# Column blocks and row blocks of the merge and the feed-forwards taken in batches of four and two

## The chip, the cores and the metric

One core of one Trainium2 chip runs the whole program. The metric is the device time of one execution in microseconds, the median of three runs. Engines are named as the profile names them: PE (TensorE, matmuls), PEld (its weight loads), DVE (VectorE), ACT (ScalarE), POOL (GpSimd), SP (the queue that starts the weight DMAs).

## The reference, cut to what matters

A block of 256 tokens with 1024 channels goes through three layers. What the change touches is the end of the first layer and the two feed-forwards of the others:

```
merged = (sigmoid(g_conv) * (yc @ w_out_conv)) + (sigmoid(g_attn) * (ya @ w_out_attn))   # first layer
out    = merged @ w_o                                                                 # 8 blocks of 128 columns
...
a, b = split(x @ w_in); a = causal conv of width 3 over tokens (a) + conv_b            # feed-forward, twice
out  = (gelu(a) * b) @ w_out                                                          # 22 blocks of 128 columns
```

All of it is f32. Each operand is split in a high and a low part (fp32r), and a product is three matmuls: high times high, low times high, high times low.

## The kernel before, in words

All weights come as one stream of 300 blocks, 128 partitions by 8 tiles of 128 columns (512 KB each), through a ring of three slots (`RING = 3`). For a block, SP starts the DMA into `raw[slot]`; ACT copies it rounded into `wh[slot]` (L396, `make_high`, once PE has used the block three before); DVE makes `wl = raw - wh` (L790, `make_low`); PE waits for that with `ready(b)`. The semaphore `used` counts the blocks that PE has finished. Every engine runs its list in order, so the refills of the ring (`refill`) are written between the other work of ACT and DVE by hand, and a refill waits where the list waits.

Two kinds of block matter here.

- A **column block** (`stationary`, L1363 to L1365) makes 128 columns of a product for all 256 tokens: 8 times three matmuls, each with its own weight load of 128 columns and 256 moving columns, into `bank[n][:, 0:256]`. Between two column blocks PE issues nothing else.
- A **row block** (`row`, `row_tile`, L1434 to L1436) multiplies a finished, activated block of 128 channels (`mh`, `ml`) with 128 rows of the output matrix: 12 matmuls of 512 moving columns, which add to the four banks 4 to 7 (`ysum`) over the whole stage.

The stages, in order. The **pairs stage** (`first(i)`, eight turns of a loop) has nine column blocks for a pair of heads: q, k, xc, then the scores, cg, bg, zc, then transposes, za, gc, then the products with the values (`pv`), ga. They go round three banks. ga is the last of a turn, q the first of the next. The **merge** has 8 products i, each of two column blocks (`mix(0)` into bank 0, `mix(1)` into bank 1) and a row block. The first **feed-forward** (f0) and the second (f1) have 22 products each: column block a(i) into bank 0, b(i) into bank 1, and row(i).

The order of the blocks in these three stages is a0, b0, then in a loop a(i+1), row(i), b(i+1), and at the end a, b and the last two rows (`last_rows`), whose second row waits until the last product is activated. a(i+1) waits until DVE has read bank 0 (`free_a`), row(i) until `ml` is made. Before the first a of the loop, four matmuls of zeros (`open_banks`, L1555) open the banks 4 to 7, since the row blocks only add. In a feed-forward a0 and b0 are made together (`two_stationary`). What lies between b(i) and row(i) is a chain: ACT `base` (L688), DVE two taps (L1270, L1273), ACT gelu (L694), DVE product with bank 1 (L1281), ACT `mh` (L698), DVE `ml` (L800). The merge has a shorter one: DVE L1040, L1047, L1051, ACT L512, DVE L1055.

During the first turns of a feed-forward, DVE also finishes the residual input (`tail_step`, four steps of 128x1024), after which POOL loads the next gains.

Of the kernel before, what the change touches and what calls it, by code (L numbers as in the profile page):

```python
# [25 lines left out]
P = 128  # L26
# [50 lines left out]
WARM_SETUP = 12  # L77
WARM_PAIR = 6
# [12 lines left out]
def slot_of(b):  # L91
    return b % RING
# [20 lines left out]
def build_program(nc, a):  # L113
    ctx = ExitStack()
    with ctx:
# [274 lines left out]
        def _(act):  # L390
# [123 lines left out]
            refill(0, B_MIX)  # L514
            refill(0, B_MIX + 1)
            merge(0)

            def products(i):
                for n in range(3):
                    refill(i, B_MIX + 2 + n)  # L520
                merge(i + 1)

            for n in range(2):
                products(n)
                if n == 0:
                    act.wait_ge(mem_in, 16)
                part = slice(n * KT // 2, (n + 1) * KT // 2)
                act.activation(memh[:, part, :], memf[:, part, :], ACT.Copy).then_inc(mem_h, 1)
            with act.Fori(2, KT - 2) as i:
                products(i)  # L530
            refill(KT - 2, B_MIX + 2)
            merge(KT - 1, 1)
            refill(KT - 2, B_MIX + 3)
            refill(KT - 2, B_MIX + 4)
# [150 lines left out]
            def ffn(ph, layer, b0):  # L685
                def base(i):

                    act.activation(t_a[:, :], bank[0][:, 0:T], ACT.Identity,  # L688
                                   bias=convf[:, layer, bass.ds(i, 1), 3], scale=convf[:, layer, bass.ds(i, 1), 2]
                                   ).then_inc(S[ph, "base"], 1)  # L690
# [5 lines left out]
                def high(i, buf=0):  # L696
                    act.wait_ge(S[ph, "m"], i + 1)
                    act.activation(mh[:, buf, :], t_c[:, :], ACT.Copy).then_inc(S[ph, "mh"], 1)  # L698

                act.wait_ge(used, b0 + 1)  # L700
                base(0)
                refill(0, b0)
                gelu(0)
                refill(0, b0 + 1)
                high(0)

                def body(i):
                    bb = b0 + 2
                    act.wait_ge(used, i * RING + (bb + 1))
                    base(i + 1)  # L710
                    refill(i, bb)
                    gelu(i + 1)
                    if isinstance(i, int):
                        high(i + 1, 1)
                        refill(i, bb + 1)
                    else:
                        refill(i, bb + 1)
                        act.wait_ge(used, i * RING + (bb + 3))
                        high(i + 1)
                    refill(i, bb + 2)  # L720

                with act.Fori(0, FT - 2) as i:
                    body(i)
                body(FT - 2)
# [59 lines left out]
        def _(dve):  # L784
# [251 lines left out]
            def part_c(i, b):  # L1036
                dve.wait_ge(used, b)
                if isinstance(i, int):
                    dve.wait_ge(S["p1", "free_act"], 5 * PAIRS1 + 5)
                dve.scalar_tensor_tensor(out=t_a[:, :].unsqueeze(1), in0=gates[:, 0, bass.ds(i, 1), :], scalar=1.0,  # L1040
                                         in1=bank[0][:, 0:T].unsqueeze(1), op0=ALU.add, op1=ALU.mult
                                         ).then_inc(S["p2", "free_a"], 1)

            def part_a(i, b, buf=0):
# [3 lines left out]
                                                 scalar=1.0, in1=bank[1][:, 0:T].unsqueeze(1),  # L1048
# [4 lines left out]
                dve.sem_inc(S["p2", "m"], 1)  # L1053
                dve.wait_ge(S["p2", "mh"], i + 1)
                dve.scalar_tensor_tensor(out=ml[:, buf, :], in0=t_c[:, :], scalar=0.5, in1=mh[:, buf, :].bitcast(F32),  # L1055
                                         op0=ALU.mult, op1=ALU.subtract).then_inc(S["p2", "ml"], 1)

            part_c(0, B_MIX + 1)
            refill(0, B_MIX)
            part_a(0, B_MIX + 2)  # L1060
            refill(0, B_MIX + 1)
            def products(i):
                part_c(i + 1, i * RING + (B_MIX + 3))
                refill(i, B_MIX + 2)
                refill(i, B_MIX + 3)
                part_a(i + 1, i * RING + (B_MIX + 5))
                refill(i, B_MIX + 4)

            for n in range(3):
                products(n)  # L1070
                if n:
                    part = slice((n - 1) * KT // 2, n * KT // 2)
                    dve.wait_ge(mem_h, n)
                    low(meml[:, part, :], memf[:, part, :], memh[:, part, :].bitcast(F32), mem_l)
            with dve.Fori(3, KT - 2) as i:
                products(i)
            part_c(KT - 1, B_KM0 - 3)
            refill(KT - 2, B_MIX + 2)
            part_a(KT - 1, B_KM0 - 2, 1)
            refill(KT - 2, B_MIX + 3)  # L1080

# [182 lines left out]
            def ffn(ph, layer, b0, nm):  # L1264
                cf = Chain(dve, dchf[layer], 1)

                def taps(i):
                    cf.begin(i)
                    dve.wait_ge(S[ph, "base"], i + 1)
                    cf.link(dve.scalar_tensor_tensor(out=t_a[:, 1:T], in0=bank[0][:, 0:T - 1],  # L1270
                                                     scalar=convf[:, layer, bass.ds(i, 1), 1], in1=t_a[:, 1:T],
                                                     op0=ALU.mult, op1=ALU.add))
                    dve.scalar_tensor_tensor(out=t_a[:, 2:T], in0=bank[0][:, 0:T - 2],  # L1273
# [4 lines left out]
                def gated(i, b, buf=0):  # L1278
                    dve.wait_ge(used, b)
                    dve.wait_ge(S[ph, "g"], i + 1)  # L1280
                    dve.tensor_tensor(t_c[:, :], bank[1][:, 0:T], t_b[:, :], ALU.mult).then_inc(S[ph, "m"], 1)  # L1281
                    dve.wait_ge(S[ph, "mh"], i + 1)
                    low(ml[:, buf, :], t_c[:, :], mh[:, buf, :].bitcast(F32), S[ph, "ml"])

                taps(0)
                refill(0, b0)
                gated(0, b0 + 2)
                refill(0, b0 + 1)

                def body(i, last=False):  # L1290
                    taps(i + 1)
                    refill(i, b0 + 2)
                    if last:
                        gated(i + 1, i * RING + (b0 + 4), 1)
                        refill(i, b0 + 3)
                    else:
                        refill(i, b0 + 3)
                        gated(i + 1, i * RING + (b0 + 5))
                        refill(i, b0 + 4)

                for n in range(4):
                    body(n)
                    tail_step(nm, n)
                with dve.Fori(4, FT - 2) as i:
                    body(i)
                body(FT - 2, True)
# [52 lines left out]
        def _(pe):  # L1359
            def stationary(slot, out, mov_h, mov_l, k0=0, k1=KT):  # L1360

                for k in range(k0, k1):
                    pe.matmul(out, wh[slot][:, k, :], mov_h(k), start=k == 0, stop=False)  # L1363
# [81 lines left out]
            def last_rows(b, first, second, half, second_made=()):  # L1445

                ready(b + 1)
                row_tile(slot_of(b), *first, 0, False, False)
# [74 lines left out]
            def first(i):  # L1523
# [28 lines left out]
            def open_banks():  # L1552

                for n in range(4):
                    pe.matmul(bank[4 + n][:, :], zeros[:, 0:P], zeros[:, :], start=True, stop=False)  # L1555


            def mix(which, slot, bk):
                stationary(slot, bk[:, 0:T], lambda k: mixh[:, which, k, :], lambda k: mixl[:, which, k, :])

            pe.wait_ge(dch1, 6 * PAIRS1)
            pe.wait_ge(S["p1", "free_act"], 5 + 5 * PAIRS1)
            open_banks()
            ready(B_MIX + 1)
            mix(0, slot_of(B_MIX), bank[0])
            ready(B_MIX + 2)
            mix(1, slot_of(B_MIX + 1), bank[1])
            with pe.Fori(0, KT - 2) as i:
                ready(i * RING + (B_MIX + 3))
                pe.wait_ge(S["p2", "free_a"], i + 1)  # L1570
                mix(0, slot_of(B_MIX + 2), bank[0])
                ready(i * RING + (B_MIX + 4))
                pe.wait_ge(S["p2", "ml"], i + 1)
                row(slot_of(B_MIX + 3), mh[:, 0, :], ml[:, 0, :], False, False)
                ready(i * RING + (B_MIX + 5))
                mix(1, slot_of(B_MIX + 4), bank[1])
            ready(B_KM0 - 3)
            pe.wait_ge(S["p2", "free_a"], KT - 1)
            mix(0, slot_of(B_KM0 - 4), bank[0])
            ready(B_KM0 - 2)  # L1580
            pe.wait_ge(S["p2", "ml"], KT - 1)
            mix(1, slot_of(B_KM0 - 3), bank[1])
            last_rows(B_KM0 - 2, (mh[:, 0, :], ml[:, 0, :]), (mh[:, 1, :], ml[:, 1, :]), S["n1", "half"],
                      ((S["p2", "ml"], KT),))
# [175 lines left out]
            def finish(ph, main, r0, half):  # L1760
# [21 lines left out]
                last_rows(r0 + 6, (oh[:, 6, :], ol[:, 6, :]), (oh[:, 7, :], ol[:, 7, :]), half, ((S[ph, "ol"], 2),))  # L1782
# [5 lines left out]
            def ffn(ph, b0, nm):  # L1788
                two_stationary(b0, nm)
                open_banks()  # L1790

# [254 lines left out]
```

## Time and profile before

| | us |
|---|---|
| median of 3 runs | 978.41 (978.02 to 979.07) |
| the profiled execution, its own time | 979.72 |
| its span, first to last instruction | 978.1 |
| PE busy | 943.0 |
| DVE busy | 664.0 |
| ACT busy | 528.0 |
| pairs stage, start of q to end of ga | 38.5 to 259.5 |
| merge | 260.6 to 329.2 |
| f0, from its first row block on | 488.9 to 665.7 |
| f1, from its first row block on | 791.7 to 968.0 |

Matmuls are pipelined, so a matmul's own duration (0.28 us for 256 columns) is longer than its distance to the next one. In what follows the distance from start to start is what counts. The granted clock of TensorE is given as a share of full speed; in each of the four stages of the table it is 1.00.

### The profile page before, as it was taken

How to read it: one execution, taken by the hardware profiler on the slowest of the kernel's cores; microseconds unless marked ns; L12 is line 12 of the kernel's file. 1: busy time of each engine (PE TensorE's matmuls, PEld its weight loads, DVE VectorE, ACT ScalarE, POOL GpSimd, SP SyncE). 2: the span in 40 equal slices, each digit the busy share in tenths (PEclk: the TensorE clock that was granted, in tenths of full speed). 3: DMA queues.
4: the chain of work that ended last, by engine and by line, in shares of the span. 5: the costliest groups of instructions: out<-in, count | busy, mean ns of one | idle time of the engine just before them, and what ended most of it. 6: DMA issues, size and time to landing. Idle time of an engine off the chain costs nothing.

```text
span 978.1 us, 19996 instructions
## 1 busy us (share of the span) xinstructions
PE 943.0 (96%) x6998; PEld 855.9 (88%) x7006; DVE 664.0 (68%) x1258; ACT 528.0 (54%) x967; POOL 65.9 (7%) x119
## 2 busy tenths in 40 slices
PE   7999999999999989989999999999999999999995
PEld 4899999999999977667899999997998689999995
DVE  5566666566666866885877666667577777666665
ACT  5455555555444557774654555556566555555552
POOL 1000000000000001560100000001000100000001
PEclk9999999999999999999999999999999999999998
DMA  7555555556555466323456655555555445655552
GB/s 246 176 184 175 187 176 177 183 167 235 181 185 188 151 205 200 111 64 105 168 186 208 208 182 189 193 190 161 198 181 164 153 150 197 219 187 192 192 183 75
DMA packets 48227, 172.90 MB, mean 177 GB/s; under 512 B 6031, under 2 KB 6479, under 8 KB 48060
## 3 DMA queue, kind: packets, MB, share of 16 engines
q1 hardware_dynamic: 44732, 159.78, 49.3%
q0 software_dynamic: 3456, 12.61, 4.3%
q8 instruction: 24, 0.39, 0.2%
q14 instruction: 15, 0.12, 0.0%
HBM read 171.29 MB, written 1.07 MB: 176 GB/s over the span
## 4 chain that ended last, share of the span: by engine, by line
PE 84%; DVE 6%; DMA 4%; ACT 2%; issue 2%; POOL 0%; SPq 0%; POOLq 0%; ACTq 0%; DVEq 0%
PE bank L1363 18%; PE bank L1364 17%; PE bank L1365 17%; PE ysum L1434 6%; PE ysum L1436 6%; PE ysum L1435 6%; DMA sb_raw<-in_stream 4%; DVE sb_wl L790 2%; PE bank L1481 2%; PE ysum L1488 2%; ACT sb_wh L396 1%; PE ysum L1495 1%; PE ysum L1411 1%; PE ysum L1412 1%; PE ysum L1415 1%
## 5 line engine op out<-in xcount | busy, mean ns | idle before, releaser
L790 DVE TENSOR_TENSOR sb_wl<-sb_raw,sb_wh 128x1024 fp32r<-128x1024 f32 x300 | 365.6, 1223 | 152.7 <-ACT sb_wh L396 151.5
L1363 PE MATMUL bank<-sb_xh,sb_wh 128*128 128x256 f32 x1360 | 383.4, 282 | 1.8 <-DVE sb_t_a L1273 1.4
L396 ACT ACTIVATE sb_wh<-sb_raw 128x1024 fp32r<-128x1024 f32 x300 | 314.8, 1054 | 126.3 <-PE ysum L1436 51.4
L1364 PE MATMUL bank<-sb_xl,sb_wh 128*128 128x256 f32 x1360 | 380.0, 279 | 0.0
L1365 PE MATMUL bank<-sb_xh,sb_wl 128*128 128x256 f32 x1360 | 380.0, 279 | 0.0
L1363 PEld LDWEIGHTS bank<-sb_xh,sb_wh 128*128 128x128 f32 x1360 | 256.2, 188 | 10.6 <-issue 4.0
L1365 PEld LDWEIGHTS bank<-sb_xh,sb_wl 128*128 128x128 f32 x1360 | 258.1, 190 | 0.0
L1364 PEld LDWEIGHTS bank<-sb_xl,sb_wh 128*128 128x128 f32 x1360 | 255.3, 188 | 1.6
L1434 PE MATMUL ysum<-sb_wh,sb_mh 128*128 128x512 f32 x208 | 81.4, 391 | 1.9 <-DVE sb_ml L800 1.2
L1436 PE MATMUL ysum<-sb_wh,sb_ml 128*128 128x512 f32 x208 | 80.9, 389 | 0.0
L1435 PE MATMUL ysum<-sb_wl,sb_mh 128*128 128x512 f32 x208 | 80.9, 389 | 0.0
L698 ACT ACTIVATE sb_mh<-sb_t_c 128x256 fp32r<-128x256 f32 x44 | 18.3, 416 | 89.5 <-DVE sb_t_c L1281 89.5
L688 ACT ACTIVATE sb_t_a<-bank,sb_convf 128x256 f32<-128x256 f32 x44 | 24.9, 566 | 47.6 <-PE bank L1365 45.1
L433 ACT ACTIVATE sb_pr<-sb_sc,sb_mx 128x128 f32<-128x128 f32 x80 | 35.5, 445 | 22.7 <-DVE sb_mx L920 22.7
L1434 PEld LDWEIGHTS ysum<-sb_wh,sb_mh 128*128 128x128 f32 x208 | 39.0, 188 | 9.5 <-issue 3.4
L1436 PEld LDWEIGHTS ysum<-sb_wh,sb_ml 128*128 128x128 f32 x208 | 39.0, 188 | 8.2
L1435 PEld LDWEIGHTS ysum<-sb_wl,sb_mh 128*128 128x128 f32 x208 | 39.0, 188 | 6.1
L1363 PE MATMUL bank<-sb_mixh,sb_wh 128*128 128x256 f32 x128 | 36.2, 282 | 0.0
L1364 PE MATMUL bank<-sb_mixl,sb_wh 128*128 128x256 f32 x128 | 36.0, 281 | 0.0
L1365 PE MATMUL bank<-sb_mixh,sb_wl 128*128 128x256 f32 x128 | 36.0, 281 | 0.0
L800 DVE TENSOR_TENSOR sb_ml<-sb_t_c,sb_mh 128x256 fp32r<-128x256 f32 x44 | 18.7, 426 | 24.2 <-ACT sb_mh L698 24.2
L1270 DVE SCALAR_TENSOR_TENSOR sb_t_a<-bank,sb_convf,sb_t_a 128x255 f32<-128x255 f32 x44 | 21.2, 481 | 18.3 <-ACT sb_t_a L688 18.2
(265 smaller groups left out, 1343.9 us busy)
## 6 DMA issues: line engine op xcount, KB each, us to landing
sb_raw<-in_stream SPq DMA_DIRECT2D x300, 512.0 KB, 3.4
sb_bias<-rel_rows POOLq DMA_DIRECT2D x12, 384.0 KB, 3.8
sb_bias<-in_alibi POOLq DMA_DIRECT2D x8, 256.0 KB, 3.1
sb_gb<-in_ln_g POOLq DMA_DIRECT2D x4, 512.0 KB, 4.8
sb_gb<-in_ln_b POOLq DMA_DIRECT2D x4, 512.0 KB, 6.5
sb_x_tok<-in_x SPq DMA_DIRECT2D x2, 512.0 KB, 3.8
sb_memf<-in_mem_t POOLq DMA_DIRECT2D x1, 1024.0 KB, 8.4
out<-sb_x_tok SPq DMA_DIRECT2D x2, 512.0 KB, 2.6
```

What stands on the lines that cost most here:

```text
L396: act.activation(wh[slot][:, :, :], raw[slot][:, :, :], ACT.Copy).then_inc(split_h, 1)
L433: act.activation(to[:, branch, h, cols], src, ACT.Exp, bias=mx[:, c:c + 1], scale=-1.0, accum_out=den[:, c:c + 1]).then_inc(S[ph, "exp"], 1)
L688: act.activation(t_a[:, :], bank[0][:, 0:T], ACT.Identity, bias=convf[:, layer, bass.ds(i, 1), 3], scale=convf[:, layer, bass.ds(i, 1), 2] ...
L790: dve.tensor_tensor(wl[slot][:, :, :], raw[slot][:, :, :], wh[slot][:, :, :].bitcast(F32), ALU.subtract).then_inc(split_l, 1)
L1270: cf.link(dve.scalar_tensor_tensor(out=t_a[:, 1:T], in0=bank[0][:, 0:T - 1], scalar=convf[:, layer, bass.ds(i, 1), 1], in1=t_a[:, 1:T], op ...
L1363: pe.matmul(out, wh[slot][:, k, :], mov_h(k), start=k == 0, stop=False)
L1364: pe.matmul(out, wh[slot][:, k, :], mov_l(k), start=False, stop=False)
L1365: last = pe.matmul(out, wl[slot][:, k, :], mov_h(k), start=False, stop=k == KT - 1)
L1434: pe.matmul(out, th[:, t * P:(t + 1) * P], hw, start=start, stop=False)
L1435: pe.matmul(out, th[:, t * P:(t + 1) * P], lw, start=False, stop=False)
L1436: last = pe.matmul(out, tl[:, t * P:(t + 1) * P], hw, start=False, stop=stop)
L1481: last = pe.matmul(outs[h][:, cols], q[r, t * P:(t + 1) * P], k[r, 0:lead + (t + 1) * P], start=True, stop=True)
```

## The change

The order becomes: four column blocks a(2j), b(2j), a(2j+1), b(2j+1) into banks 0 to 3, then row(2j-1), then row(2j). The stream of weights is laid out in that order. `open_banks` goes; the first row block starts its banks itself (`start=True`). The first batch of the merge waits, bank by bank, only for what last read that bank, and no longer for all of the pairs stage. The first matmul of some column blocks is issued as two: in the first block of every later batch as 192 and 64 columns, and in every ga of the pairs stage as 128 and 128. On DVE the making of `ml` is a step of its own, after the refill that follows the product; on ACT the odd product's `mh` waits in every batch but the first for the row block of the last odd product. The first two batches of a feed-forward hold the four tail steps, one for each product.

```diff
+SPLIT = 192
...
-            def stationary(slot, out, mov_h, mov_l, k0=0, k1=KT):
+            def stationary(slot, out, mov_h, mov_l, k0=0, k1=KT, split=0):
                 for k in range(k0, k1):
-                    pe.matmul(out, wh[slot][:, k, :], mov_h(k), start=k == 0, stop=False)
+                    if split and k == 0:
+                        pe.matmul(out[:, 0:split], wh[slot][:, k, :], mov_h(k)[:, 0:split], start=True, stop=False)
+                        pe.matmul(out[:, split:T], wh[slot][:, k, :], mov_h(k)[:, split:T], start=False, stop=False)
+                    else:
+                        pe.matmul(out, wh[slot][:, k, :], mov_h(k), start=k == 0, stop=False)
...
-                    stationary(slot_of(B_FIRST + p), bank[p % 3][:, 0:T], xm, xml)
+                    stationary(slot_of(B_FIRST + p), bank[p % 3][:, 0:T], xm, xml, split=P if kind == "ga" else 0)
...
+            def batches(ph, b0, count, column, half):
+                def column_free(i, n):
+                    if n > 1:
+                        pe.wait_ge(S[ph, "free_a" if n == 2 else "m"], i)
+                def row_made(b, i, c, start=False):
+                    ready(b)
+                    pe.wait_ge(S[ph, "ml"], i + 1)
+                    row(slot_of(b0 + (4 if start else 4 - c)), mh[:, c, :], ml[:, c, :], start, False)
+                def four(j):
+                    for n in range(4):
+                        ready(j * 6 + (b0 + n))
+                        column_free(j * 2, n)
+                        column(n, slot_of(b0 - 1 + n), SPLIT if n == 0 else 0)
+                row_made(b0 + 5, 0, 0, True)
+                with pe.Fori(1, count // 2 - 1) as j:
+                    four(j)
+                    row_made(j * 6 + (b0 + 4), j * 2 - 1, 1)
+                    row_made(j * 6 + (b0 + 5), j * 2, 0)
+                four(count // 2 - 1)
+                row_made(b0 + 3 * count - 2, count - 3, 1)
+                last_rows(b0 + 3 * count - 2, (mh[:, 0, :], ml[:, 0, :]), (mh[:, 1, :], ml[:, 1, :]), half,
+                          ((S[ph, "ml"], count - 1),), ((S[ph, "ml"], count),))
+            p1a, p1d = S["p1", "free_act"], S["p1", "free_dve"]
+            for n, made in enumerate((((dch1, 6 * PAIRS1 - 1), (p1d, 4 * PAIRS1 + 5)),
+                                      ((dch1, 6 * PAIRS1), (p1a, 5 * PAIRS1 + 4)),
+                                      ((p1a, 5 * PAIRS1 + 5),), ())):
...
+                mix(n % 2, slot_of(B_MIX + n), bank[n])
+            batches("p2", B_MIX, KT, lambda n, slot, split: mix(n % 2, slot, bank[n], split), S["n1", "half"])
...
             def ffn(ph, b0, nm):
                 two_stationary(b0, nm)
-                open_banks()
...
+                pe.wait_ge(kv_free, 4)
+                for n in range(2, 4):
+                    ready(b0 + n + 1)
+                    stationary(slot_of(b0 + n), bank[n][:, 0:T], xm, xml)
+                batches(ph, b0, FT, lambda n, slot, split: stationary(slot, bank[n][:, 0:T], xm, xml, split=split),
+                        S["n3", "half"])
```

DVE's list in a feed-forward afterwards (ACT's is alike: `base`, refill, gelu, refill, `mh`, and after the odd product two more refills):

```diff
+                def products(j):
+                    fixed = isinstance(j, int)
+                    b = b0 if fixed and j == 0 else b0 - 1
+                    for c in range(2):
+                        i = j * 2 + c
+                        taps(i, c)
+                        refill(j, b + 2 * c, 6)
+                        gated(i, j * 6 + (b + 2 * c + 2), c)
+                        refill(j, b + 2 * c + 1, 6)
+                        gated_low(i, c)
+                        if c:
+                            refill(j, b + 4, 6)
+                            if not fixed or 0 < j < FT // 2 - 1:
+                                refill(j, b + 5, 6)
+                        if fixed and j < 2:
+                            tail_step(nm, 2 * j + c)
```

## Rows read from the trace of the kernel before

**Rows 1.** The page: busy time of the engines over the span, and instructions.
```profile
PE 943.0 (96%) x6998; PEld 855.9 (88%) x7006; DVE 664.0 (68%) x1258; ACT 528.0 (54%) x967; POOL 65.9 (7%) x119
```

**Rows 2.** Busy by stretch, f0: window, length, PE, PEld, DVE, ACT, POOL, PEclk, DMA, GB/s.
```profile
488.00:661.00 173.00, 172.17 (x1234) 162.25 (x1233) 116.15 (x151) 89.66 (x127) 1.13 (x2) 1.00 0.59 194
```

**Rows 3.** Timeline of PE, pairs stage: first matmuls of consecutive blocks (start, duration).
```profile
41.30 0.28 PE L1363 MATMUL bank<-sb_xh,sb_wh 128*128 128x256 f32 x1
44.02 0.28 PE L1363 MATMUL bank<-sb_xh,sb_wh 128*128 128x256 f32 x1
...
65.91 0.28 PE L1363 MATMUL bank<-sb_xh,sb_wh 128*128 128x256 f32 x1
68.74 0.28 PE L1363 MATMUL bank<-sb_xh,sb_wh 128*128 128x256 f32 x1
```

**Rows 4.** Timeline of PE, f0: a block, the next block, the row block.
```profile
567.66 0.28 PE L1363 MATMUL bank<-sb_xh,sb_wh 128*128 128x256 f32 x1
...
570.49 0.28 PE L1363 MATMUL bank<-sb_xh,sb_wh 128*128 128x256 f32 x1
...
573.32 0.39 PE L1434 MATMUL ysum<-sb_wh,sb_mh 128*128 128x512 f32 x1
```

**Rows 5.** Timeline of PE, f0: a block that starts after an idle stretch, its follower.
```profile
536.97 0.38 PE L1363 MATMUL bank<-sb_xh,sb_wh 128*128 128x256 f32 x1 [0.38 <-DVE sb_wl L790]
537.19 0.28 PE L1364 MATMUL bank<-sb_xl,sb_wh 128*128 128x256 f32 x1
...
539.81 0.39 PE L1434 MATMUL ysum<-sb_wh,sb_mh 128*128 128x512 f32 x1
```

**Rows 6.** The chain of waits, merge: start, duration; eight transposes of 128 columns.
```profile
334.73 0.87 PE ysum L1470 x8
```

**Rows 7.** Timeline of PE, scores: matmuls of 128 columns of unsplit f32.
```profile
46.83 0.37 PE L1481 MATMUL bank<-sb_k_s,sb_q_s 64*128 64x128 f32 x1
...
47.04 0.27 PE L1481 MATMUL bank<-sb_k_s,sb_q_s 64*128 64x128 f32 x1
```

**Rows 8.** Timeline of PE, from the last ga into the merge.
```profile
259.41 0.28 PE L1365 MATMUL bank<-sb_xh,sb_wl 128*128 128x256 f32 x1
260.56 0.81 PE L1555 MATMUL ysum<-sb_zeros 128*128 128x512 bf16 x3 [0.87 <-ACT sb_gates L501]
...
261.33 0.28 PE L1364 MATMUL bank<-sb_mixl,sb_wh 128*128 128x256 f32 x1
```

**Rows 9.** Timeline of PE, last two row blocks of the merge and of f0.
```profile
323.94 0.39 PE L1436 MATMUL ysum<-sb_wh,sb_ml 128*128 128x512 f32 x1
...
325.30 0.39 PE L1435 MATMUL ysum<-sb_wl,sb_mh 128*128 128x512 f32 x1
...
661.01 0.39 PE L1436 MATMUL ysum<-sb_wh,sb_ml 128*128 128x512 f32 x1
...
661.87 0.39 PE L1435 MATMUL ysum<-sb_wl,sb_mh 128*128 128x512 f32 x1
```

**Rows 10.** Timeline, start of f0: PE's zeros, DVE, first row block.
```profile
483.23 1.23 DVE L790 TENSOR_TENSOR sb_wl<-sb_raw,sb_wh 128x1024 fp32r<-128x1024 f32 x1
483.75 0.55 PEld L1555 LDWEIGHTS ysum<-sb_zeros 128*128 128x128 bf16 x4
...
489.24 0.39 PE L1435 MATMUL ysum<-sb_wl,sb_mh 128*128 128x512 f32 x1
```

**Rows 11.** Timeline, start of f1: DVE, PE's last matmuls of a0 and b0, first row block.
```profile
785.97 1.23 DVE L790 TENSOR_TENSOR sb_wl<-sb_raw,sb_wh 128x1024 fp32r<-128x1024 f32 x1
786.08 0.63 PE L1381 MATMUL bank<-sb_xl,sb_wh 128*128 128x256 f32 x4
...
792.04 0.39 PE L1435 MATMUL ysum<-sb_wl,sb_mh 128*128 128x512 f32 x1
```

**Rows 12.** The page's groups: ACT's part of a refill (count, busy us, mean ns).
```profile
L396 ACT ACTIVATE sb_wh<-sb_raw 128x1024 fp32r<-128x1024 f32 x300 | 314.8, 1054 | 126.3 <-PE ysum L1436 51.4 <-PE bank L1365 32.6 <-DMA sb_raw<-in_stream 25.1
```

**Rows 13.** Busy by stretch, early (columns as in rows 2), where the granted clock was low.
```profile
20.00:23.30 3.30, 3.30 (x9) 2.59 (x8) 1.42 (x2) 0.00 (x0) 0.00 (x0) 0.50 0.74 263
```

More of the change, by code:

```diff
@@ L512, in merge @@
                 act.activation(mh[:, buf, :], t_c[:, :], ACT.Copy, scale=0.5).then_inc(S["p2", "mh"], 1)
[L514 to L525, printed above, removed]
-                    act.wait_ge(mem_in, 16)
[L527 to L534, printed above, removed]
+            for j in range(KT // 2):
+                b = 6 * j + B_MIX - (j > 0)
+                refill(0, b)
+                refill(0, b + 1)
+                merge(2 * j, 0)
+                refill(0, b + 2)
+                refill(0, b + 3)
+                if j:
+                    act.wait_ge(used, b + 5)
+                merge(2 * j + 1, 1)
+                refill(0, b + 4)
+                if j:
+                    refill(0, b + 5)
+                if j == 0:
+                    act.wait_ge(mem_in, 16)
+                if j < 2:
+                    part = slice(j * KT // 2, (j + 1) * KT // 2)
+                    act.activation(memh[:, part, :], memf[:, part, :], ACT.Copy).then_inc(mem_h, 1)
             def refills(b0, n):
@@ L1282, in gated @@
                     dve.wait_ge(S[ph, "mh"], i + 1)
[L1283 to L1306, printed above, removed]
+                    low(ml[:, c, :], t_c[:, :], mh[:, c, :].bitcast(F32), S[ph, "ml"])
+                def products(j):
+                    fixed = isinstance(j, int)
[8 more added lines that the diff above has]
+                        if c:
+                            refill(j, b + 4, 6)
+                            if not fixed or 0 < j < FT // 2 - 1:
+                                refill(j, b + 5, 6)
+                        if fixed and j < 2:
+                            tail_step(nm, 2 * j + c)
@@ L1308, in _ @@
+                for j in range(2):
+                    products(j)
+                with dve.Fori(2, FT // 2 - 1) as j:
+                    products(j)
+                products(FT // 2 - 1)
             ffn("f0", 0, B_FFN0, "n2")
@@ L1443, in row, with last_rows @@
                 last.then_inc(used, 1)
-            def last_rows(b, first, second, half, second_made=()):
+            def last_rows(b, first, second, half, first_made=(), second_made=()):
                 ready(b + 1)
+                for made in first_made:
+                    pe.wait_ge(*made)
                 row_tile(slot_of(b), *first, 0, False, False)
@@ L1550, in _ @@
             first(PAIRS1 - 1)
[L1552 to L1562, printed above, removed]
-            open_banks()
-            ready(B_MIX + 1)
@@ L1565, in _ @@
[L1565 to L1584, printed above, removed]
+            def mix(which, slot, bk, split=0):
+                stationary(slot, bk[:, 0:T], lambda k: mixh[:, which, k, :], lambda k: mixl[:, which, k, :],
+                           split=split)
@@ L1905, in skewed @@
     def skewed(n, first, second, rows):
[L1906 to L1914 removed]
+        for j in range(0, n, 2):
+            for i in (j, j + 1):
+                add(_columns(first, i * P))
+                add(_columns(second, i * P))
+            for i in (j - 1, j):
+                if i >= 0:
+                    add(rows[i * P:(i + 1) * P])
         add(rows[(n - 1) * P:n * P])
```

149 lines of the change are left out of this document (61 added, 88 removed).

## The prediction

> **What bounds the kernel.** I read the busy times of the page first: PE is busy for 943.0 of 978.1 us, DVE for 664.0 and ACT for 528.0 [rows 1]. Only what shortens PE's list or fills its gaps can move the time. The busy times by stretch say the same of a feed-forward: PE 172.17 of 173.00 us, DVE 116.15, ACT 89.66, granted clock 1.00 [rows 2]. So inside the loops there is almost no wait to take away, and what the change can win lies (a) in how densely PE's matmuls follow each other, and (b) in the gaps at the seams of the stages. For (a) the view is the timeline of PE with its starts. A column block of 24 matmuls comes in two lengths: 44.02 - 41.30 = 2.72 us and 68.74 - 65.91 = 2.83 us, with the same instructions, tiles and clock [rows 3]. I call them fast (113 ns a matmul) and slow (118 ns). The reader is to see that nobody waits for another engine in either: it is a rhythm between weight loads and matmuls, and it stays as it is from block to block until something disturbs PE. In the feed-forward the block behind a row block is slow, and the one after it: 570.49 - 567.66 and 573.32 - 570.49, both 2.83 [rows 4]. That row stands for 46 such seams in merge, f0 and f1; none of them leads into a fast block. In the pairs stage ga, q, k, xc are slow (ga starts behind the value products) and cg to gc fast (behind the scores or the transposes).
>
> **The change part by part** (against the profiled execution, 979.72 us; it is 1.31 above the median of 978.41, which I take off at the end).
>
> *Seam into the merge.* Before, PE's last ga matmul starts at 259.41, the zeros wait 0.87 for ACT's gates, and the second mix matmul starts at 261.33 [rows 8]. Two steps of 0.12 would have brought it to 259.65. The new first mix block waits only for the last low part of the convolution and for bank 0, both long done. Gain 1.68. Next late: the weights of the third block, since ACT refills that slot only behind ga; its two copies take 1.05 [rows 12] and 1.23 us and end some 3 us behind ga, and two blocks of 2.72 cover them.
>
> *Start of f0 and f1.* Before, from the zeros' weight load at 483.75 to the second matmul of row(0) at 489.24 it takes 5.49 us [rows 10], for a column block (2.83) and one row matmul (0.23): 2.43 too long, by the zeros, the wait for DVE's taps and that for `ml`. Now a1 and b1 follow at once into free banks. What is late next is a1's weights: DVE makes them from 483.23 to 484.46 [rows 10]. That is 0.71 behind 483.75; with the hand-over of 0.08 and a restart, which costs 0.22 instead of 0.12 for the first step [rows 5], 0.89 stays lost. Gain 1.54. In f1 the last of four matmuls from 786.08 ends its slot at 786.55, row(0) is at 792.04, DVE ends at 787.20 [rows 11]: 2.43 before, 0.65 + 0.18 = 0.83 after, gain 1.60. DVE gets a tail step of 1.2 us between the first and second product; following its list by hand, the weights of a2 are then done within 0.3 us of the time at which PE wants them. I leave that at nothing, and keep 0 to 0.3 for each.
>
> *Ends.* The last row block waits for the chain of the last product: 325.30 - 323.94 = 1.36 where two row matmuls take 0.45, so 0.91 in the merge, and 0.86 - 0.45 = 0.41 in f0 [rows 9]; f1 repeats f0 (a gap of the same 0.41 at its end). Now a whole row block (2.72) lies between. The chain takes longer, since ACT's `mh` waits for that row block: about 3.8 us behind b, against 4.1 when PE wants it. Gain 0.91 + 0.82 = 1.73, between 1.4 and 1.73.
>
> The seams give 1.68 + 1.54 + 1.60 + 1.73 = 6.55 us.
>
> *In the loops* the same instructions are issued in another order. Cover for the refills: a slot has two blocks of PE (5.4 us) from its release; ACT's copy, DVE's subtraction and the elementwise work before them end some 3 us (column) to 3.3 us (row block, whose `mh` now stands ahead) after it. Nothing waits. The one wait for weights in f0's loop (0.38 named, [rows 5]) comes with a gains load; it may stay or go: 0, bounds -0.5 and +0.5. The moved `ml` feeds a row block at least two column blocks later.
>
> *The split matmuls.* There are 8 in the pairs, 3 in the merge, 10 in each feed-forward: 31. No row shows an fp32r matmul below 256 columns, so I bound it. From below: every matmul has its own weight load, and transposes of 128 columns, each with one, follow at 0.87 / 8 = 0.109 us [rows 6]; two pieces cost 0.22 instead of 0.12, +0.10. From above: a narrow unsplit f32 matmul at 0.21 (47.04 - 46.83, [rows 7]), two pieces 0.42, +0.30. I take 0.10, because the loads are the same as the transposes'. The other end: 31 x 0.20 = 6.2 us more.
>
> The Trainium skill, "TensorE: Matmul & The Clock Gate", section "Back-to-back issue gap", gives N / 2.4 + 2.5 ns for a matmul alone; by it the pieces of 192 and 64 columns would take 112 ns together and the splits would be free, some 3 us less than my sum. The same page's "LDWEIGHTS" gives 107 ns for 128 columns, and the 0.109 of the transposes agrees with that, not with the first formula.
>
> *What the split does to the rhythm* is the largest term. Behind a row block the first matmul finds its weights loaded long ago, and the run falls into the slow rhythm, 46 times of 46. A narrow first piece ends before the next load does, so PE starts the following matmul right behind a load, as after an idle stretch. Such restarts mostly lead to the fast rhythm: 539.81 - 537.19 = 2.62 us for 23 matmuls in f0, 114 ns each [rows 5]. In the pairs all 16 starts behind scores and transposes are fast and all 8 behind the value products slow; of 24 other restarts in the timeline 17 are fast. Two kinds of split, each with one place and one outcome: I take both as working. Then ga, q, k, xc become fast: 8 + 7 x 3 = 29 blocks. The merge has 16 (the first batch follows ga, without a row block between), f0 40 and f1 41 that are now slow. 126 x 0.11 = 13.9 us. Off go 31 x 0.10 for the pieces and 31 x 0.04 for settling and for the first row matmuls behind a fast block: 4.3. Net 9.6. Bounds: if no split works, the loss is 3.1. Batches of four matter here only since they need half as many splits.
>
> Sum: 6.5 + 9.6 = 16.1. 979.72 - 16.1 = 963.6; at the median 978.4 - 16.1 = 962.3.
>
> **Rivals.** *Only the 192/64 split works:* 93 x 0.11 - 23 x 0.14 - 8 x 0.10 = 6.2, with the seams 12.7: 965.7. *Only ga's works:* 33 x 0.11 - 8 x 0.14 - 23 x 0.10 = 0.2, with the seams 6.7: 971.7. Against both: neither has a precedent in the trace, and ga starts where 8 of 8 are slow. *No split works,* a change that doesn't do what its split says: 6.5 - 3.1 = 3.4: 975.0. For it: a third of the restarts are slow, and the steps that decide differ by a few ns. *Slower: narrow pieces are dear and don't change the rhythm.* Each costs 0.30 [rows 7], 31 of them 9.3 against 6.5: 981.2. It decides from 0.21 us a split on; for it speaks the only narrow matmul not a transpose, against it the loads, which set the pace of transposes of the same width.
>
> *The clock falls in the batches.* Four banks in turn instead of two, with a fresh group in each. The trace has the low level of 1.2 GHz at 20.0 to 23.3, behind a wait: 9 row-sized matmuls in 3.30 us [rows 13], 0.41 apart as I count it, against 0.23 at 2.4 GHz. One such stretch in each of 26 batches costs 26 x 3.3 x (1 - 0.23 / 0.41) = 38 us: about 1000. Against it: the pairs stage goes round three banks with the clock at 1.00, and in the new loops PE never waits. The Trainium skill names this mechanism in the same page's section "A second HAM failure mode: psum-queue depth-cycling"; this trace doesn't bear it out.
>
> **How the numbers follow.** Both splits work 0.52; only 192/64 0.12; only ga's 0.12; none 0.16; slower by dear pieces 0.06; clock 0.02. The forecast is 962.3, its own range 960 to 964.5. To hold 8 in 10 the range must reach over the partial cases to that without rhythm: 960 to 975.5. About 0.2% (2 us) is what a measurement here tells from no change. Faster by more than that: all of the first three and most of the fourth, 0.89; within 0.2%: 0.04; slower: 0.07.
>
> **What would show it.** Timeline of PE: column blocks 2.72 us apart in merge and feed-forwards, a batch of six blocks 16.5 instead of 16.75; the two pieces 0.11 apart each; a turn of the pairs stage 27.4 instead of 27.66. No zeros; the first mix matmul 0.12 behind ga; f0's a1 at DVE's `wl`; no gap before the last rows. Wrong if blocks behind a split are 2.83 long, if the pieces lie 0.2 apart, or if PE waits for `wl` once in each batch.

## The result, and the profile after

The changed kernel takes 963.21 us, the median of 4 runs (962.44 to 963.91), beside 978.21 for the kernel before (976.5 to 979.07, 4 runs). The ratio is 0.9844, 95% interval 0.9832 to 0.9857: 15.0 us faster. The forecast was 962.3, within 960.0 to 975.5. The profiled execution of the changed kernel took 963.07 us with a span of 961.4; before it was 979.72 and 978.1.

Busy times of the page, which answer to [rows 1], and the pairs stage, f0 and f1 by stretch, of which the row of f0 answers to [rows 2] (columns: window, length, then busy us and instructions of PE, PEld, DVE, ACT, POOL, then granted clock, DMA share, GB/s):

```profile
PE 929.3 (97%) x7025; PEld 844.3 (88%) x7025; DVE 659.2 (69%) x1258; ACT 527.7 (55%) x967; POOL 65.4 (7%) x119
```

```profile
37.00:258.00 221.00, 221.00 (x1928) 213.43 (x1927) 143.73 (x274) 117.16 (x218) 10.05 (x18) 1.00 0.57 188
...
477.00:655.00 178.00, 177.50 (x1295) 166.88 (x1296) 120.55 (x162) 96.90 (x134) 1.37 (x4) 1.00 0.62 198
774.00:958.00 184.00, 176.82 (x1287) 165.60 (x1286) 124.92 (x166) 96.38 (x134) 4.45 (x6) 0.99 0.56 181
```

PE's busy time fell by 13.7 us though it runs more matmuls: inside the loops it hardly ever waited, it was slow. The granted clock is 1.00, 1.00 and 0.99 there, so the rival in which it falls is out: PE goes round four banks, and the clock stays at its upper level, 2.4 GHz. The Trainium skill names such a fall ("TensorE: Matmul & The Clock Gate", section "A second HAM failure mode: psum-queue depth-cycling"); no run of this case shows it.

Timeline of PE in f0 (start, duration, line): a batch, from its split block over the next block to the row block and on to the next batch. It answers to [rows 4].

```profile
552.09 0.25 PE L1364 MATMUL bank<-sb_xh,sb_wh 128*128 128x192 f32 x1
552.18 0.21 PE L1365 MATMUL bank<-sb_xh,sb_wh 128*128 128x64 f32 x1
552.23 0.36 PE L1368 MATMUL bank<-sb_xl,sb_wh 128*128 128x256 f32 x1
552.43 0.28 PE L1369 MATMUL bank<-sb_xh,sb_wl 128*128 128x256 f32 x1
...
563.09 0.39 PE L1438 MATMUL ysum<-sb_wh,sb_mh 128*128 128x512 f32 x1
...
568.55 0.25 PE L1364 MATMUL bank<-sb_xh,sb_wh 128*128 128x192 f32 x1
```

Four column blocks take 563.09 - 552.09 = 11.00 us where four slow ones took 4 x 2.83 = 11.32, and the whole batch 16.46 (forecast 16.5). From the first piece to the second whole matmul it is 552.43 - 552.09 = 0.34 us, where two whole matmuls in the slow rhythm take 0.235: the split costs 0.104 against them, as priced. Counting all blocks of at least twelve 256-column matmuls in the timeline, 135 of 200 were slow before (118 ns a matmul) and 17 are now.

The same view in the pairs stage, ga's start in one turn and the next; then the seam into the merge, against [rows 8]:

```profile
62.01 0.33 PE L1364 MATMUL bank<-sb_xh,sb_wh 128*128 128x128 f32 x1
...
89.36 0.33 PE L1364 MATMUL bank<-sb_xh,sb_wh 128*128 128x128 f32 x1
89.52 0.27 PE L1365 MATMUL bank<-sb_xh,sb_wh 128*128 128x128 f32 x1
...
256.31 0.28 PE L1369 MATMUL bank<-sb_xh,sb_wl 128*128 128x256 f32 x1
256.43 0.28 PE L1367 MATMUL bank<-sb_mixh,sb_wh 128*128 128x256 f32 x1
```

A turn is 89.36 - 62.01 = 27.35 us, and mix starts 0.12 behind ga, with nothing between. The start of f0, against [rows 10] (DVE's weights, then PE), and the last two row blocks of f0, against [rows 9]:

```profile
476.13 1.23 DVE L789 TENSOR_TENSOR sb_wl<-sb_raw,sb_wh 128x1024 fp32r<-128x1024 f32 x1
...
477.50 0.36 PE L1367 MATMUL bank<-sb_xh,sb_wh 128*128 128x256 f32 x1 [0.67 <-DVE sb_wl L789]
...
652.87 0.39 PE L1438 MATMUL ysum<-sb_wh,sb_mh 128*128 128x512 f32 x1
653.10 0.39 PE L1439 MATMUL ysum<-sb_wl,sb_mh 128*128 128x512 f32 x1
```

Only the wait for `wl` is left at the start, and the last rows are 0.23 apart with no gap. Setting the same marks in both timelines gives the ledger. The marks are the first pair block, the end of the last ga, the first memory key block, the end of a0 and b0 and so on; the end of a block is here the start of its last matmul and one step of 0.11 to 0.12 on it.

| stage | before | after | moved | forecast |
|---|---|---|---|---|
| up to the first pair block | 38.45 | 37.47 | -0.98 | 0 |
| pairs | 221.08 | 218.96 | -2.12 | -2.1 |
| merge with its seam | 69.67 | 65.71 | -3.96 | -3.9 |
| f0 with its start and end | 181.97 | 176.89 | -5.08 | -5.0 |
| f1 with its start and end | 181.41 | 176.90 | -4.51 | -5.1 |
| all between and behind | | | 0.0 | 0 |

The first line is chance. The first pair block starts anywhere from 36.86 to 39.45 in the profiled executions below. So I give for each kernel the rest, its span less that start: 939.6 before, 923.9 after, 15.7 less where 16.1 was forecast.

Two places are not as forecast, and in f0 they hide each other. The first is the wait in the middle of f0, which the forecast left at nothing. Before, PE's last two steps around it were:

```profile
536.31 0.28 PE L1365 MATMUL bank<-sb_xh,sb_wl 128*128 128x256 f32 x1
536.97 0.38 PE L1363 MATMUL bank<-sb_xh,sb_wh 128*128 128x256 f32 x1 [0.38 <-DVE sb_wl L790]
```

That is 0.66 where 0.12 would do. In the changed f0 loop no step of PE is longer than 0.25, so some 0.5 us more are won than forecast. The second is the second batch of f0 (DVE first, then PE):

```profile
482.46 1.22 DVE L895 TENSOR_TENSOR sb_x_tok<-sb_z,sb_gb 128x1024 f32<-128x1024 f32 x1
...
484.51 1.22 DVE L789 TENSOR_TENSOR sb_wl<-sb_raw,sb_wh 128x1024 fp32r<-128x1024 f32 x1
...
485.54 0.39 PE L1440 MATMUL ysum<-sb_wh,sb_ml 128*128 128x512 f32 x1
485.78 0.36 PE L1364 MATMUL bank<-sb_xh,sb_wh 128*128 128x192 f32 x1
485.97 0.22 PE L1365 MATMUL bank<-sb_xh,sb_wh 128*128 128x64 f32 x1
```

The first line is the norm's tail step. It pushes a2's `wl` to 485.73, just when PE wants it, and PE starts some 0.01 us late. That is nothing, but the first piece now stands alone for 0.19 us instead of 0.09, and the four blocks of this batch, like those of the batch at 783.51 in f1, which starts 0.06 late, are slow. Four slow blocks cost 4 x 0.107 = 0.43. In f0 the wait that went makes up for them, and -5.08 agrees with the forecast only by that; f1 has the slow batch alone, and moved by 0.6 less than forecast.

### The profile page after: what moved, and what is told of

Read it like the earlier page. It is cut to its first block, busy times and chain, and to the rows that moved or that the text cites. A ratio compares the mean times of both kernels' runs of the same rounds, so it can differ in the third digit from the quotient of the medians.

```text
span 961.4 us, 19777 instructions
## 1 busy us (share of the span) xinstructions
PE 929.3 (97%) x7025; PEld 844.3 (88%) x7025; DVE 659.2 (69%) x1258; ACT 527.7 (55%) x967; POOL 65.4 (7%) x119
## 4 chain that ended last, share of the span: by engine, by line
PE 83%; DVE 7%; ACT 3%; DMA 3%; issue 2%; POOL 0%; SPq 0%; POOLq 0%; DVEq 0%; ACTq 0%
PE bank L1368 18%; PE bank L1369 18%; PE bank L1367 18%; PE ysum L1438 6%; PE ysum L1440 6%; PE ysum L1439 6%; DMA sb_raw<-in_stream 3%; DVE sb_wl L789 2%; PE bank L1487 1%; PE ysum L1494 1%; PE ysum L1501 1%; ACT sb_wh L397 1%; PE ysum L1415 1%; PE ysum L1416 1%; PE ysum L1419 1%
## 5 line engine op out<-in xcount | busy, mean ns | idle before, releaser
L1369 PE MATMUL bank<-sb_xh,sb_wl 128*128 128x256 f32 x1360 | 376.1, 277 | 0.0
L1367 PE MATMUL bank<-sb_xh,sb_wh 128*128 128x256 f32 x1332 | 370.7, 278 | 1.3 <-DVE sb_wl L789 1.3
L1367 PEld LDWEIGHTS bank<-sb_xh,sb_wh 128*128 128x128 f32 x1332 | 250.1, 188 | 6.3 <-issue 4.0
L919 DVE CUSTOM_DVE_ANT_0 sb_sc<-bank,sb_bias 128x128 f32<-128x128 f32 x76 | 22.7, 351 | 15.1 <-PE ysum L1487 13.1
```

Of the source, the lines that this page charges most:

```text
L919: dve.tensor_tensor_reduce(sc[:, branch, h, s384(t)], src[:, cols], add, 1.0, guard, ALU.add, ALU.min, mx[:, c:c + 1]).then_inc(S[ph, "max ...
L1369: last = pe.matmul(out, wl[slot][:, k, :], mov_h(k), start=False, stop=k == KT - 1)
```

## The experiments

Theory A: any narrow first piece sets the fast rhythm, because it ends before the next load does. Rival B: the rhythm depends on the exact moment at which the first whole matmul starts. Rival C: the order (batches, zeros gone) brings the rhythm. First, four kernels take the change apart; the kernel before took 978.45 beside them (11 runs).

**No splits.** The changed kernel with both kinds of split taken out:

```diff
-  stationary(slot_of(B_FIRST + p), bank[p % 3][:, 0:T], xm, xml, split=P if kind == "ga" else 0)
+  stationary(slot_of(B_FIRST + p), bank[p % 3][:, 0:T], xm, xml)
-  column(n, slot_of(b0 - 1 + n), SPLIT if n == 0 else 0)
+  column(n, slot_of(b0 - 1 + n), 0)
```

> The changed kernel with every first matmul whole again: batches and seams alone. My theory (the splits make the fast rhythm; 117 blocks are fast by them in the changed kernel's trace, 0.107 us each, and a split costs 0.14): 963.2 + 117 x 0.107 - 31 x 0.14 = 971.4, that is about 6.8 us below before (the seams, forecast 6.5). Column blocks of ga to xc and of all batches 2.83 us long. Rival (the rhythm comes from the four banks and the order of the batches, and the splits only cost): the blocks stay at 2.72 and the time falls to 963.2 - 3.2 = 960.0.

Measured: 971.94 us (969.76 to 974.06), ratio 0.9936 [0.9916, 0.9956]. The order and the seams alone give 6.5 us. Its f0, first matmuls of a batch:

```profile
556.91 0.28 PE L1367 MATMUL bank<-sb_xh,sb_wh 128*128 128x256 f32 x1
...
559.74 0.28 PE L1367 MATMUL bank<-sb_xh,sb_wh 128*128 128x256 f32 x1
```

559.74 - 556.91 = 2.83: slow, and 137 of 200 blocks are. C falls.

**Only ga's split, and only the 192/64 split.** One of the two edits above each time.

> The split of ga alone, none in the batches. Theory: the pairs' ga, q, k, xc and the merge's first four blocks stay fast (33 blocks), 84 become slow: 963.2 + 84 x 0.107 - 23 x 0.14 = 969.0. Rival (either split enough, the rhythm then holding over row blocks): about 960.8, the price of 23 splits less than the changed kernel.

> The 192/64 split alone, ga whole. Theory: 33 blocks slow again: 963.2 + 33 x 0.107 - 8 x 0.14 = 965.6. Rival (ga's split does nothing that lasts, since scores and transposes follow anyway): 962.4, eight splits less.

Measured: 969.12 (ratio 0.9907 [0.989, 0.9924]) and 966.38 (0.9877 [0.9859, 0.9895]). Against 971.94, ga's split is worth 2.8 and the other 5.6 us; both together 8.7. Slow blocks: 96 and 42. Each split works in its own stage: with ga's alone no block of the pairs stage is slow and 36 and 42 of 42 are in f0 and f1; with the other alone 29 are slow in the pairs stage, and 2 and 0 in f0 and f1.

**Splits in the old order.** The kernel before, with ga cut at 128 and the column block behind each row block cut at 192:

```diff
-  stationary(slot_of(B_FIRST + p), bank[p % 3][:, 0:T], xm, xml)
+  stationary(slot_of(B_FIRST + p), bank[p % 3][:, 0:T], xm, xml, split=P if kind == "ga" else 0)
-  mix(1, slot_of(B_MIX + 4), bank[1])
+  mix(1, slot_of(B_MIX + 4), bank[1], 192)
-  stationary(slot_of(b0 + 4), bank[1][:, 0:T], xm, xml)
+  stationary(slot_of(b0 + 4), bank[1][:, 0:T], xm, xml, split=192)
```

> The kernel before, its order and seams kept, with the splits put in: ga as 128/128, and the column block that follows each row block as 192/64 (6 in the merge, 20 in each feed-forward). Theory (rhythm is a matter of what stands right ahead of a block, not of batches): each of the 46 splits makes the two blocks up to the next row block fast, 46 x (2 x 0.107 - 0.14) = 3.4, and ga's makes 32 blocks fast for 8 splits, 2.3: 978.2 - 5.7 = 972.5. Rival (batches of four are needed): 978.2 - 2.3 + 46 x 0.10 = 980.5.

Measured: 972.5, ratio 0.9943 [0.9926, 0.9959]. Its merge, a split block, the next and the row block:

```profile
270.34 0.25 PE L1364 MATMUL bank<-sb_mixh,sb_wh 128*128 128x192 f32 x1
270.43 0.21 PE L1365 MATMUL bank<-sb_mixh,sb_wh 128*128 128x64 f32 x1
...
273.18 0.28 PE L1367 MATMUL bank<-sb_mixh,sb_wh 128*128 128x256 f32 x1
...
275.90 0.39 PE L1438 MATMUL ysum<-sb_wh,sb_mh 128*128 128x512 f32 x1
```

275.90 - 273.18 = 2.72: fast. The split needs no batches; only 5 blocks of 200 are slow. But there are 54 splits instead of 31. The rest of the span is 932.3 against 923.9, some 8.3 more: 23 splits at 0.104 + 0.02 are 2.9, the 12 blocks that are fast here and slow there give back 1.3, and 6.8 is left for the seams, where the forecast had 6.55.

In the next session the width of the piece, the tail steps and the place of the cut were changed (before: 977.78, 11 runs).

**128 instead of 192, and 64 instead of 192.** `SPLIT = 128`, `SPLIT = 64`, nothing else:

> The changed kernel with 128/128 in place of 192/64 in the 23 batches. Theory A (any narrow first piece will do: it ends before the next weights are loaded, PE then starts right behind a load): the blocks stay at 2.72, 963.2 within 0.5. Theory B (the width sets a phase, and 192 is one that lands in the fast rhythm): 128 lands in the slow one with a chance of about one half, then 84 blocks are slow again: 963.2 + 84 x 0.107 - 0.7 = 971.5.

> The same with 64/192: the narrow piece first. Theory A: 963.2 within 0.5, blocks of 2.72. Theory B: again even odds of about 971.5; widths that differ in their result would show that it is the width.

Measured: 962.72 (ratio 0.9841 [0.9824, 0.9857]) and 971.0 (0.9928 [0.9909, 0.9946]). The second is the prediction's rival *only ga's works* come true, at 971.7 by its working. PE at the start of a batch with 128, then with 64:

```profile
519.65 0.22 PE L1364 MATMUL bank<-sb_xh,sb_wh 128*128 128x128 f32 x1
...
519.82 0.33 PE L1368 MATMUL bank<-sb_xl,sb_wh 128*128 128x256 f32 x1
519.99 0.28 PE L1369 MATMUL bank<-sb_xh,sb_wl 128*128 128x256 f32 x1
```

```profile
521.87 0.19 PE L1364 MATMUL bank<-sb_xh,sb_wh 128*128 128x64 f32 x1
...
522.07 0.30 PE L1368 MATMUL bank<-sb_xl,sb_wh 128*128 128x256 f32 x1
522.21 0.28 PE L1369 MATMUL bank<-sb_xh,sb_wl 128*128 128x256 f32 x1
```

Theory A falls: the 64-column piece is the narrowest and its batches are slow. The second whole matmul starts 0.34 behind the first piece with every width (519.99 - 519.65, 522.21 - 521.87, and 552.43 - 552.09 with 192). What differs is when the first whole one starts, and so how long it lasts before the second: 0.17 with 128 and 0.20 with 192, 0.14 with 64.

**Tail steps one batch later.** DVE's norm steps in batches 1 and 2 instead of 0 and 1:

```diff
-                        if fixed and j < 2:
-                            tail_step(nm, 2 * j + c)
+                        if fixed and 0 < j < 3:
+                            tail_step(nm, 2 * j - 2 + c)
...
-                for j in range(2):
+                for j in range(3):
...
-                with dve.Fori(2, FT // 2 - 1) as j:
+                with dve.Fori(3, FT // 2 - 1) as j:
```

> The changed kernel with DVE's four tail steps of each feed-forward in the second and third batch instead of the first and second. Theory: the weights of a2 then come before PE wants them, the wait ahead of batch 2 goes (0.01 us in f0, 0.06 in f1), and with it the accident that this batch runs slow (8 blocks of 2.83): 963.2 - 8 x 0.107 - 0.07 = 962.3. Rival (the slow batch has another cause, the first row block with its opened banks, say): the four blocks stay at 2.83 and the time at 963.1.

Measured: 962.43 (959.82 to 965.94), ratio 0.9845 [0.9821, 0.9869]. The second batch of f0, DVE's `wl` and PE's start:

```profile
484.21 1.22 DVE L789 TENSOR_TENSOR sb_wl<-sb_raw,sb_wh 128x1024 fp32r<-128x1024 f32 x1 [0.15 <-ACT sb_wh L397]
...
486.15 0.39 PE L1440 MATMUL ysum<-sb_wh,sb_ml 128*128 128x512 f32 x1
486.37 0.25 PE L1364 MATMUL bank<-sb_xh,sb_wh 128*128 128x192 f32 x1
486.46 0.21 PE L1365 MATMUL bank<-sb_xh,sb_wh 128*128 128x64 f32 x1
```

The weights are ready 0.94 before PE needs them, the pieces lie as everywhere else, and both batches are fast: 7 slow blocks of 200, and a rest of 922.1, 1.8 below the changed kernel's, where ten slow blocks fewer and twice 0.10 for the first piece account for 1.3. So the tail step makes the late start. That a late start makes a slow batch is not shown. The kernel with the 192/64 split alone has the early tail steps too, and its second batch of f1 starts 0.05 late, with pieces of the same length as at 485.78:

```profile
787.81 0.35 PE L1364 MATMUL bank<-sb_xh,sb_wh 128*128 128x192 f32 x1
788.00 0.22 PE L1365 MATMUL bank<-sb_xh,sb_wh 128*128 128x64 f32 x1
...
790.76 0.28 PE L1367 MATMUL bank<-sb_xh,sb_wh 128*128 128x256 f32 x1
...
793.48 0.28 PE L1367 MATMUL bank<-sb_xh,sb_wh 128*128 128x256 f32 x1
```

793.48 - 790.76 = 2.72: fast. In the medians the 0.8 between the changed kernel and this one is within the scatter.

**Cut in the row block.** The last row matmul before each batch in 320 and 192 columns, the column block whole:

```diff
+                    if cut and t == n == 1:
+                        pe.matmul(out[:, 0:cut], tl[:, t * P:(t + 1) * P], hw[:, 0:cut], start=False, stop=False)
+                        last = pe.matmul(out[:, cut:512], tl[:, t * P:(t + 1) * P], hw[:, cut:512], start=False, stop=stop)
...
+                        cut=0 if c else 320)
...
-  column(n, slot_of(b0 - 1 + n), SPLIT if n == 0 else 0)
+  column(n, slot_of(b0 - 1 + n), 0)
```

> The column blocks of the batches whole; in their place the last matmul of the row block ahead of them is issued as 320 and 192 columns. Theory A: what matters is a matmul shorter than a weight load right ahead of the column block; 320 columns cover the second piece's load, so a cut costs 0.142 + 0.109 - 0.227 = 0.024 instead of 0.10: 963.2 - 23 x 0.08 = 961.4. Rival (the narrow piece must stand inside the column block, with the same weights): the 84 blocks are slow, 963.2 + 84 x 0.107 - 23 x 0.12 = 969.4.

Measured: 970.24, ratio 0.9917 [0.9894, 0.9939]; 100 blocks slow.

```profile
505.40 0.30 PE L1441 MATMUL ysum<-sb_wh,sb_ml 128*128 128x320 f32 x1
505.54 0.25 PE L1442 MATMUL ysum<-sb_wh,sb_ml 128*128 128x192 f32 x1
505.63 0.30 PE L1367 MATMUL bank<-sb_xh,sb_wh 128*128 128x256 f32 x1
505.77 0.28 PE L1368 MATMUL bank<-sb_xl,sb_wh 128*128 128x256 f32 x1
```

Here the first whole matmul lasts 0.14, as with 64, and the blocks are slow as with 64. A narrow piece just ahead of the block is not enough.

In the last session (before: 978.52, 12 runs) the border was looked for, the cut was moved, and the best version was run.

**A first piece of 96 columns.** `SPLIT = 96`:

> The changed kernel with pieces of 96 and 160 columns instead of 192 and 64 (ga keeps 128). Splits of 128 and 192 led to the fast rhythm (962.7 and 963.2), one of 64 didn't (971.0). Theory: the width of the first piece decides, by the moment at which the first whole matmul starts against the load behind it, and the border lies somewhere between 64 and 128. If 96 is on the side of 128: 962.5 to 963.5, column blocks behind the split 2.72 apart. If it is on the side of 64: 970.5 to 971.5, blocks 2.83 apart. No time between is expected, since a block that is slow stays slow; a time between would say that the rhythm is not of two kinds only. Rival, that only widths of at least 128 columns in the piece that comes first count: 971.

Measured: 973.6 (970.62 to 978.08, 7 runs), ratio 0.9962 [0.9943, 0.9981].

```profile
553.78 0.21 PE L1364 MATMUL bank<-sb_xh,sb_wh 128*128 128x96 f32 x1
553.83 0.30 PE L1365 MATMUL bank<-sb_xh,sb_wh 128*128 128x160 f32 x1
553.97 0.32 PE L1368 MATMUL bank<-sb_xl,sb_wh 128*128 128x256 f32 x1
554.12 0.28 PE L1369 MATMUL bank<-sb_xh,sb_wl 128*128 128x256 f32 x1
```

The side of 64: 96 slow blocks, first whole matmul 0.15. At an undisturbed start the border lies between 96 and 128. Why the median is 2 us above its forecast stays open; the profiled execution, 970.62, was its fastest and lay on it.

**The cut in the middle of a block.** The 192/64 split on the fifth k step of the second column block of each batch:

```diff
-                    if split and k == 0:
+                    if split and k == at:
...
-  column(n, slot_of(b0 - 1 + n), SPLIT if n == 0 else 0)
+  column(n, slot_of(b0 - 1 + n), SPLIT if n == 1 else 0)
```

with `at=4` in the merge and the feed-forwards, 0 for ga.

> The changed kernel, but the 192/64 split of each batch stands on the fifth of the eight k steps of its second column block instead of on the first matmul of the first. Theory: the slow rhythm is a state that any disturbance of the right size ends, wherever it stands. Then each batch has one and a half slow blocks before the split and two and a half fast ones behind it: 26 batches less those that are fast anyway, 24 x 1.5 x 0.107 = 3.9 us above the changed kernel, 967.1. Rival: the split works only at the place where PE comes from a row block, because it keeps the slow rhythm from starting; in the middle of a slow block it does nothing, and costs 0.10 in each: the time with ga's split alone, 969.1, and 23 x 0.10 on it, 971.5.

Measured: 966.89 (965.12 to 968.21), ratio 0.9884 [0.9866, 0.9901].

```profile
539.96 0.28 PE L1367 MATMUL bank<-sb_xh,sb_wh 128*128 128x256 f32 x1
...
541.25 0.28 PE L1369 MATMUL bank<-sb_xh,sb_wl 128*128 128x256 f32 x1
541.37 0.25 PE L1364 MATMUL bank<-sb_xh,sb_wh 128*128 128x192 f32 x1
541.46 0.21 PE L1365 MATMUL bank<-sb_xh,sb_wh 128*128 128x64 f32 x1
...
541.94 0.28 PE L1368 MATMUL bank<-sb_xl,sb_wh 128*128 128x256 f32 x1
...
542.85 0.28 PE L1367 MATMUL bank<-sb_xh,sb_wh 128*128 128x256 f32 x1
```

Before the cut (541.37 - 539.96) / 12 = 0.118 a matmul, behind it (542.85 - 541.94) / 8 = 0.114, in the same block and in the two after it. Nothing but PE's own stream changed there. So the slow rhythm is a state of that stream, and a cut of 192 and 64 columns ends it here too, in the middle of a block with no row block ahead of it; other places within a block were not tried.

**The best version.** Tail steps late, 128/128 everywhere, and the same cut on slow blocks outside the loops, nine more splits in all (the memory keys of both layers of attention have three calls each):

```diff
-SPLIT = 192
+SPLIT = 128
...
-  stationary(slot_of(pair_at(n)), bk[:, 0:T], xm, xml)
+  stationary(slot_of(pair_at(n)), bk[:, 0:T], xm, xml, split=P if n in (1, 7) else 0)
-  stationary(slot_of(b + n), bank[n][:, 0:T], xm, xml)
+  stationary(slot_of(b + n), bank[n][:, 0:T], xm, xml, split=0 if i or n else P)
```

with `split=P` for the memory keys too.

> The version to which the runs point: the tail steps of the norm in the second and third batch, pieces of 128 and 128 everywhere, and the same split on six more blocks outside the loops that are slow in the trace with later tail steps (the two memory key blocks, second and eighth pair block, first query block of the last attention; the key block in its two halves). Against the changed kernel's 963.2: the first batches of f0 and f1 fast, -0.8; seven slow blocks at most turned, 5 x 0.107 less 5 x 0.10 for their splits, 0 to -0.3. Expected 962.2, between 961.5 and 962.8. Rival, that the extra splits only cost: 963.0.

Measured: 962.67 (961.88 to 967.47), ratio 0.9848 [0.9825, 0.9871], 6 slow blocks. No better than late tail steps alone (rest 922.6 against 922.1): a split costs 0.10, about as much as the one block that it turns. In its trace the first three blocks of the pairs stage are slow, which no edit touched; that is 0.3 of the 0.5 between the two.

## Why the prediction was right

- **Rhythm.** Right in kind and size. A turned block gives 2.83 - 2.72 = 0.11 and a split costs 0.104 where 0.10 was taken. Only the first row matmuls behind a fast block add some 0.02, where 0.04 was taken with the settling. The net was forecast at 9.6. The kernel without splits is 8.7 above the changed one in the medians, and 931.7 - 923.9, about 7.7, in the rest of the span. By blocks it should be 120 x 0.107 - 31 x 0.124 = 9.0; the difference between 7.7 and 9.0 is not explained. The 120 fewer slow blocks, not 126, are 32 in the pairs stage (29 forecast), 16 in the merge, 38 in f0 (40) and 32 in f1 (41), and 2 elsewhere. Two batches stay slow, 6 blocks of f1 are fast without any split, and the first three of the pairs stage are slow there by chance.
- **Its reason.** Wrong in part. The prediction said that a narrow first piece ends before the next load, and that this makes the rhythm. With 64 and 96 columns it does so even earlier, and the rhythm stays slow. That 192 and 128 were both on the good side was luck of the width, not understood; "the steps that decide differ by a few ns" described it better than the step taken. Of the theories B is left, as what goes along with the outcome at undisturbed starts; it is not a cause that was shown.
- **Seams.** Right: 6.8 by the kernel with the old order, 6.5 in the medians without splits, against 6.55. At f0's start a1 comes 0.83 late and its first step is 0.08 longer (0.19 for 0.11), 0.91 lost where 0.89 was reckoned. The wait for weights in the middle of f0, put at nothing within 0.5 either way, went too and gave some 0.5: luck, which covers the slow batch there.
- **Tail step.** The place that was costed at nothing, with 0 to 0.3 for each start. The wait itself is 0.01 and 0.06, as forecast, but in this kernel both batches behind it are slow: 2 x 4 x 0.107 = 0.86. What failed is the reckoning that a stall of some ns can cost only those ns; it need not cost more, as the fast batch at 787.81 shows.
- **Price of the pieces.** 0.104, near the row for the transposes and far from 0.30. The formula of the Trainium skill ("TensorE: Matmul & The Clock Gate", section "Back-to-back issue gap"), by which the pieces would be free, is stated there for a matmul alone, and the same section says that in a stream with a weight load for each matmul both set the spacing. The trace agrees with the latter: behind the first piece at 552.09 the loads start at 552.10, 552.20 and 552.32, about 0.11 apart.
- **Batches.** "Batches of four matter here only since they need half as many splits" holds for the rhythm. They also bring the ends and starts.

## What to carry to other kernels

Where an engine is busy all the time, compare the pitch of equal instructions from block to block: two pitches for the same work are time to be had without moving anything else. If matmuls with a weight load each come in two pitches, try one matmul in two pieces behind the block that sets the slow one, and try several widths, since the wrong one costs the split and brings nothing. A cut pays only where several blocks follow it undisturbed, so put such blocks one behind the other, and keep weights well ahead of the cut.

## What the runs showed of the hardware

- Fp32r matmuls of 256 columns with a load of 128 columns each run at 113 or 118 ns, at the same granted clock, for as long as nothing disturbs them. In the undisturbed batches it goes with the time from the first whole matmul behind the pieces to the next: 0.14 (64 columns, cut row) and 0.15 (96) lead to 118, 0.17 (128) and 0.20 (192) to 113.
- That isn't a full rule. The first piece of 192 behind a late start lasts 0.19, its whole matmul still 0.20, and its batch is slow twice (485.78 and 783.51 in the changed kernel) and fast once (787.81 with 192/64 alone). With 64 columns the two batches whose weights come just in time, at 488.44 and 789.59, are fast, and so are the two with 96 columns, at 486.61 and 787.67; all the other batches that begin with such a piece are slow. So a width of 128 or more isn't the rule either. What decides between load and matmul is finer than these records, and stays open; that the weight loads are involved at all is argued from their pitch, since no kernel without them was tried.
- Chance alone moves places that no edit touched: the first three blocks of the pairs stage are slow in 5 of the 13 profiled executions and fast in 8, its start moves by 2.6 us over them, and in the first attention the stretch from 371.55 to 395.44 with 96 columns took 23.9 us, the same stretch with 64 took 27.1. So a few blocks more or less between two timelines can be chance; where all the batches of a stage turn, it isn't.
